# An eighth weight home and a last expert added on the chip in a two-layer mixture-of-experts kernel

## What is computed

```python
def expert_choice_ffn(h, router_w, router_b, w_gate, w_up, w_down):
    cap = EC_CAPACITY * n // N_EXPERTS            # 64 latent rows, 32 context rows
    affinity = jax.nn.softmax(h @ router_w + router_b)
    gates, idx = lax.top_k(jnp.swapaxes(affinity, 1, 2), cap)
    xg = h[idx]
    hid = silu(xg @ w_gate[e]) * (xg @ w_up[e])
    y = (hid @ w_down[e]) * gates[..., None]
    return zeros.at[idx].add(y)                   # summed over the experts

for l in range(DEPTH):                            # DEPTH = 2
    ...
    f_l = expert_choice_ffn(modulate(rmsnorm(x, norm_ffn_pre[l]), mod_l[3], mod_l[4]), ...)
    x = x + mod_l[5] * rmsnorm(f_l, norm_ffn_post[l])
    if l < DEPTH - 1:                             # the context takes part in layer 0 only
        ctx = ctx + mod_c[5] * rmsnorm(expert_choice_ffn(..ctx..), norm_ffn_post[l])
return x
```

## Time and profile before

| | |
|---|---|
| median of 3 executions | 2183.53 us (2183.09 to 2184.22) |
| the profiled execution, its own time | 2187.91 us |
| its span, first to last instruction | 2186.1 us |
| mean granted clock of TensorE | 0.943 of full speed |
| PE busy | 1913.0 us, 88% |
| DVE busy | 633.0 us, 29% |
| ACT busy | 504.2 us, 23% |
| POOL busy | 208.6 us, 10% |

### The profile page before, as it was taken

One profiled execution on the slowest core, in us unless ns is written; L12 is line 12 of the kernel. 1 busy time (PEld: TensorE's weight loads), 2 busy tenths in 40 slices (PEclk: granted clock), 3 DMA queues, 4 the chain that ended last, 5 costly groups with the idle time before them and its releaser, 6 DMA issues. The chain is left out here.

```text
span 2186.1 us, 25132 instructions
## 1 busy us (share of the span) xinstructions
PE 1913.0 (88%) x10556; PEld 916.3 (42%) x10556; DVE 633.0 (29%) x1195; ACT 504.2 (23%) x999; POOL 208.6 (10%) x225
## 2 busy tenths in 40 slices
PE   5998999989979999999995999999694978778775
PEld 2656555434423333333333766655342323222221
DVE  2257542352331111111105356523523100000002
ACT  3145541442200000000005145514221100000002
POOL 2300000210011110111111000001100100000000
PEclk9999999989989999999997999999796999888988
DMA  9520305111279999999998123014317999999997
GB/s 350 165 77 1 135 1 180 52 41 76 90 296 400 394 395 399 394 399 395 395 395 307 39 77 135 1 60 172 136 47 292 403 398 406 401 400 406 401 401 268
DMA packets 166976, 534.51 MB, mean 245 GB/s; under 512 B 11208, under 2 KB 19730, under 8 KB 166866
## 3 DMA queue, kind: packets, MB, share of 16 engines
q1 hardware_dynamic: 148720, 487.40, 57.3%
q0 software_dynamic: 16480, 40.21, 6.5%
q10 hardware_dynamic: 1666, 5.31, 0.7%
HBM read 507.72 MB, written 25.17 MB: 244 GB/s over the span
## 5 line engine op out<-in xcount | busy, mean ns | idle before, releaser
L2766 PE MATMUL ps<-ring,arena 128*64 128x512 f32 x1040 | 244.6, 624 | 36.2 <-DMA ring<-in_w_up 33.1
L2766 PE MATMUL ps<-arena 128*64 128x512 f32 x840 | 199.4, 626 | 36.4 <-DMA arena<-in_w_up 36.4
L2105 PE MATMUL ps<-arena,ring 128*128 128x256 f32 (+1 forms) x640 | 202.8, 479 | 5.9 <-DMA ring<-in_w_in 3.0
L2105 PEld LDWEIGHTS ps<-arena,ring 128*128 128x128 f32 x640 | 123.2, 194 | 86.3 <-issue 70.1
L2766 PEld LDWEIGHTS ps<-ring,arena 128*64 128x64 f32 x1040 | 79.5, 143 | 188.5 <-issue 184.8
L2023 DVE TENSOR_TENSOR arena<-arena,ps 128x512 f32<-128x512 f32 x32 | 22.0, 687 | 439.7 <-ACT arena L1302 439.7
L2614 PE MATMUL ps<-ring,arena 128*128 128x512 f32 x320 | 142.8, 601 | 2.2 <-DVE arena L1940 1.8
L789 POOL DMA_INDIRECT expert_sums<-arena,small x32 | 51.6, 1611 | 839.2 <-ACT arena L1309 839.2
L2766 PEld LDWEIGHTS ps<-arena 128*64 128x64 f32 x840 | 64.3, 144 | 160.2 <-issue 160.2
L1302 ACT ACTIVATE arena<-ps 128x512 f32<-128x512 f32 x32 | 19.1, 597 | 453.9 <-PE ps L2766 453.9
L2809 PE MATMUL ps<-ring,arena 128*64 128x512 f32 x496 | 111.3, 594 | 2.8 <-DMA ring<-in_w_down 2.1
(11 more groups left out here) (352 smaller groups left out, 2404.5 us busy)
## 6 DMA issues: line engine op xcount, KB each, us to landing
ring<-in_w_up SPq DMA_DIRECT2D x33, 2048.0 KB, 18.4
ring<-in_w_gate SPq DMA_DIRECT2D x32, 2048.0 KB, 23.3
ring<-in_w_down SPq DMA_DIRECT2D x31, 2048.0 KB, 24.5
ring<-in_ada_w SPq DMA_DIRECT2D x24, 2048.0 KB, 12.9
arena<-in_w_down SPq DMA_DIRECT2D x21, 2048.0 KB, 25.2
arena<-in_w_gate SPq DMA_DIRECT2D x19, 2048.0 KB, 22.7
arena<-in_w_up SPq DMA_DIRECT2D x18, 2048.0 KB, 17.1
ring<-in_w_in SPq DMA_DIRECT2D x6, 2048.0 KB, 15.9
```

Of the source, the lines that this page charges most:

```text
L2105: ins = mm(o[0:n, c0:c1], w[:, k, col:col + n], hT[:, k, c0:c1], start=k == 0, stop=k == KD - 1)
L2766: ins = mm(px[0][hf * 64:hf * 64 + 64, col:col + 512], xl[e % 2][:, at:at + CAP_L], w[c][:, hf * 512:hf * 512 + 512], start=b + c == 0, st ...
```

## The change

It has six parts. (1) In layer 0, `tail_job` has another order. (2) Layer 0 gets an eighth home. It consists of three pieces, one of them `mrows`, which the mixing stage still uses, so that its first load waits for ACT's and DVE's marks after the choice of rows; `sg_l` and one of two `hT_l` go. (3) PE's first experts in layer 0 come in another order. (4) POOL adds an expert's context rows ahead of its latent rows, and DVE modulates the context rows of expert 1 ahead of the latent rows of expert 0. (5) In layer 1 gate blocks are let go on a semaphore of their own, `gate_used`, after the gate products and not after the up products. (6) At the end of layer 1 the sums of 15 experts are loaded from HBM. The sixteenth's rows are added by products: for each tile of 128 tokens PSUM receives identity x sums plus a 0/1 matrix x rows, where the matrix (`last_hits`) compares numbers of slots (`last_no`, loaded from the constants) with the row's number. ACT and DVE read the sum from PSUM. The last gate's rows are formed before the last down stage.

```diff
-XRING = [RING + EXTRA] * (DEPTH - 1) + [len(LAST_HOMES)]
+XRING = [RING + EXTRA + 1] * (DEPTH - 1) + [len(LAST_HOMES)]
...
-        order += [("mix", c + 1)] * (c + 1 < n) + [("ctx", 0)] * (early and c == 3) + [("out", c)]
-        order += [("turn", c - 1)] * (c >= 1) + [("ctx", c - 3)] * (early and c > 3)
+        order += [("mix", c + 1)] * (c + 1 < n) + [("ctx", 0), ("ctx", 1)] * (early and c == 4) + [("out", c)]
+        order += [("turn", c - 1)] * (c >= 1) + [("ctx", 2)] * (early and c == 4)
...
-            let_go += [("blocks_used", n)] * 2 + [("gu_lat", e + 1)] * 2
+            if l < DEPTH - 1:
+                let_go += [("blocks_used", n)] * 2 + [("gu_lat", e + 1)] * 2
+            else:
+                let_go += [("gate_used", 2 * e + 1), ("blocks_used", n), ("gate_used", 2 * e + 2), ("gu_lat", e + 1)]
...
+        extra_homes = [((0, 4, extra[i]),) for i in range(EXTRA)]
+        extra_homes += [((0, 2, ar(20480, 2048)), (2, 3, mrows[:, :]), (3, 4, ar(m0 + 3584, 1024)))]
...
-                    elif home == "d":
+                    elif home == "d" or (l < DEPTH - 1 and home == RING + EXTRA):
                         for s in (dve_ph, act_ph):
                             sp.wait_ge(s, PHASES * l + CHOICE_DONE)
...
-                pool.wait_ge(S["y_lat"], l * NE + e + 1)
-                pool.indirect_dma_start(halves_sum[l], at_rows(e, 0), y_l[e % 2], None, compute_op=ALU.add)\
-                    .then_inc(put_lat, 16)
                 if ctx_on:
                     pool.wait_ge(S["y_ctx"], l * NE + e + 1)
                     pool.indirect_dma_start(quarters_sum[l], at_rows(e, NE), y_c[e % 2], None, compute_op=ALU.add)\
                         .then_inc(put_ctx, 16)
+                pool.wait_ge(S["y_lat"], l * NE + e + 1)
+                pool.indirect_dma_start(halves_sum[l], at_rows(e, 0), y_l[e % 2], None, compute_op=ALU.add)\
+                    .then_inc(put_lat, 16)
...
-                add_rows(l, NE - 1)
+                    if l == DEPTH - 1 and e == NE + 1:
+                        pool.wait_ge(S["down_lat"], l * NE + NE - 2)
+                        load(last_no, T["const"][:, K_END:K_END + SEQ], s_no)
+                if l < DEPTH - 1:
+                    add_rows(l, NE - 1)
...
                 latent_rows_turned(0)
+                if ctx_on:
+                    pe.wait_ge(S["rows_mod"], n0 + 2)
+                    pe.wait_ge(S["hid_ctx"], n0 + 1)
+                    n = BLOCKS[l].index((0, 1, 0))
+                    context_gate_up(1, 0, block(n), block(n + 1))
...
+                def last_sums_up(i, t):
+
+                    o, no = last_sums(t), last_hits[:, i * P:(i + 1) * P]
+                    pe.wait_ge(sum_loaded[t], 16 * (l + 1))
+                    for hf in range(2):
+                        mm(o[:, hf * 512:(hf + 1) * 512], ident, Fa[:, t, hf * 512:(hf + 1) * 512], start=True, stop=False)
+                    pe.wait_ge(S["y_lat"], n0 + NE)
+                    for hf in range(2):
+                        half = slice(hf * CAP_L, (hf + 1) * CAP_L)
+                        ins = mm(o[:, hf * 512:(hf + 1) * 512], no[half, :], y_l[(NE - 1) % 2][half, :], start=False, stop=True)
+                    ins.then_inc(S["sums_full"], 1)
```

183 lines of the change are left out of this document (108 added, 75 removed).

## The result

The changed kernel takes 2189.55 us (median of 20 executions, 2182.92 to 2196.21); the kernel before, in 20 executions beside it, 2184.65 us. The ratio is 1.0021, with a 95% interval of 1.0013 to 1.0029: slower by some 4.6 us, where I had forecast no difference (2183.0, range 2176 to 2189). The change moves the time little, but not because it does little: in the profiled executions (spans 2186.07 and 2189.55) it gives 12.6 us away in one place and gets 9.1 back, net, in the others.

The account below looks back on a forecast made before the run. In layer 0's experts PE and the weight stream were taken to run neck and neck, in layer 1's the stream alone; 11.9 - 2.85 - 1.1 - 3.5 - 5.0 = -0.55 from 2183.53 gave 2183.0 us, range 2176 to 2189.

Parts of the forecast that it names:

- Term A: Start of layer 0's experts: PE waits for block 7 and block 12 is issued late; 11.9 us slower.
- T: Layer 0's start: the moment when the first half of `gate_up(0)` ends, forecast at 646.8 us.
- doesn't repay it: Layer 0's experts: an eighth home gives nothing to a stream whose DMA share is 1.03.
- Term B: Tail of layer 0: the third `out_half` loses its slot wait and the half clock behind it; 2.85 us faster.
- Term C: Handover to layer 1: the context's scatter-add, issued ahead of the latent one, leaves the chain; 1.1 us faster.
- Term D: Layer 1's start: gate blocks let go after gate products restart the stream sooner; 3.5 us faster.
- Term E: End of layer 1: sums of 15 experts loaded early, the last rows added by products; 5.0 us faster.
- Last rows 2163.0: End of layer 1: the last rows come at 2163.0 us, the constants' load costing the stream 0.6, hidden.
- The end gives little: Rival, end of layer 1: slow fifteenth scatter-add or half-clock products, gain only 1.8 to 3 us; 15 in 100.
- Layer 0 stays bound by PE: Rival, layer 0's experts: only PE's own shift counts, +4.6 us, time 2175.7 us; 25 in 100.
- Block 7 lands late: Rival, layer 0's start: block 7 lands after 634.4 us, at 643.4 giving 2192.0 us; 15 in 100.
- the gate semaphore does nothing: Rival, layer 1's start: the earlier release gains 0, time 2186.6 us, no difference; 5 in 100.

Follow-up runs that it names:

- seven homes: The basis, but layer 0 has seven homes as before; 2176.92 us, ratio 0.9961.
- the basis: The changed kernel with PE's old order at layer 0's start and the last gate's rows ahead of the last up stage; 2174.15 us, ratio 0.9949.
- gate with up: The basis, but in layer 1 the gate blocks are let go with the up blocks again; 2174.76 us, ratio 0.9953.
- old end: The basis, but with the end of layer 1 as before: sixteen scatter-adds, sums loaded after the last, no products; 2174.64 us, ratio 0.9955.
- layer 0 only: The basis, but with layer 1's gate blocks let go with the up blocks and its end as before; 2179.14 us, ratio 0.9964.
- early gate rows: The changed kernel with the last gate's rows ahead of the last up stage and DVE's diagonal before the 0/1 matrix; 2186.78 us, ratio 0.9992.

## Why the prediction was wrong

**Term A (11.9) was right, in mechanism and size.** 12.6 measured, the landing of block 7, T and the issue of block 12 within 0.2 us of the forecast (PE's wait was 5.1 and not 6.1, because PE came to it a microsecond later), and the two orders tried apart give their shares. What it lacked: 1.0 us because the context's down ran slower than in the earlier trace rows; and the sentence that the eighth home "doesn't repay it" is wrong at the handover, where seven homes bring the sums' load 1.9 us later ("seven homes" against the basis).

**Term B's tail (2.85)** came as forecast (2.95). The cut by itself moves by more than that, but the rows bear it out: the wait of 1.85 is gone, the third `out_half` took 8.80 us before and takes 7.03 now, and the wait that I had put at 0.7 is found at 0.64:

```profile
557.95 7.11 PE L2647 MATMUL ps<-ring,arena 128*128 128x512 f32 x16 [0.64 <-ACT arena L1268]
```

But 0.5 to 1.7 of it is lost again at the context's down, which I had booked nowhere.

**Term C (1.1)** gave 2.1 at the sums' first load (10.84 and 8.75 us behind the last down), 0.8 at the opening products of layer 1 and 0.4 up to its experts; tried alone, the order of the scatter-adds is worth 1.6 at the sums' load.

**Term D (3.5)** gave 4.7; half clock had lengthened before's group more than after's (9.89 against 8.62). At like clock it gives 3.45, in two pairs of kernels (10.10 and 6.65; 8.49 and 5.04).

**Term E (5.0) is the step that failed**: 1.8 at the end, less 0.75 for the constants' load, which I had called hidden. From the first waiting load to the last up stage the three kernels without that load took 450.4 to 450.6 us, all others 451.1 to 451.8. From the last weighting to the first square the term was right: 4.38 us (forecast 4.65) where it was 9.65, 5.27 gained. What failed stands on either side of it. "Last rows 2163.0" let the stream set the last down; in the changed kernel PE sets it, and the last weighting starts 26.1 us after the cut at the last up stage and not 24.0, 2.1 later. And "DVE's chain behind it, 2.46 us a tile, stays": it goes at PE's pace of up to 2.98, and from the first square to the end it takes 1.35 more. 2.13 + 1.35 - 5.27 is the -1.79 of the table.

Under both lies one misreading. The sentence was "the first tile then takes four products. At full clock (0.43 each)". I had taken "x4" in the row of the gate rows for four products. `gate_rows` has two, as the order's rows do (x2): the trace keeps two records for each float32 product of 128 rows by 512 columns. At full clock one takes 0.98, not 0.43 (L2901: 1.95 for two). So the gate rows hold PE for 1.98 us and not 0.9, and a tile takes 2.95 and not 1.7, which is more than DVE's 2.46. The Trainium skill, "FP8 and Floating Point Precision", section "TensorE Precision Notes", says that a true float32 product passes the array four times; as an estimate, 4 x 512 columns at 2.4 GHz are 0.85 us, which is near L2901's 0.98 and would have caught the misreading. The two products of the 0/1 matrix, with 64 rows each, take 1.06 together, about half as much (from 2172.20 to 2173.26): they read different halves of the rows. The Trainium skill, "TensorEngine Tiling (Array Packing)", section "When to Use Tiling", names a contract dimension of 64 as a case for two tiles of rows; the 1.06 agrees with it.

The half clock in the last up stage, 1.7 us, is the other half of the late last down. Of the 14 profiled kernels nine had it, and before's, the basis, "gate with up", "old end" and "layer 0 only" had not. By itself it costs 0.1 us at the last down (with early gate rows), because PE then merely waits less for blocks 94 and 95. The gate rows alone at full clock would cost an estimated 0.4 (26.1 less 1.7, against 23.9 to 24.0); no run shows that. Both together are more than those waits can take up.

**The rivals.** "The end gives little" had the right place and nearly the right size (-1.8 to -3), but the wrong cause: the products ran at full clock, and the fifteenth scatter-add took 4.8 us, not 8.0. "Layer 0 stays bound by PE" has fallen for the changed kernel; in the windows from 700 to 1150 us the stream stood at 392 to 401 GB/s, as before, and not at the ceiling of the ports, 435 GB/s in the Trainium skill, "DMA: Bandwidth & Descriptors", section "Where 436 GB/s comes from". "Block 7 lands late" and "the gate semaphore does nothing" have fallen. The sum with E at its measured size, 2183.0 + 4.0 = 2187.0, would have been inside the range; 2.5 us remain, of which 0.7 is term A and the rest lies within what the medians of before moved from one series of measurements to another (2184.65 to 2187.76).

**Open:** the timing gives the release and the old end 1 us each, the traces 3.45 and 4.3, and for both together 3 to 5 stand against 7. With the uncertainty of 4 these don't contradict each other, and only more executions of each kernel would tell. Why one execution has half clock in the last up stage and another not is open, too.

## What to carry to other kernels

When a stream of loads is within a per cent of the engine that it feeds, ask of each reordering which home it lets go later, and find the first load that waits for it: one home let go 17 us later cost 6 us, and with the second reorder, which made PE wait for block 7, it was 12.6, though PE had the same work. A stream's last block matters beyond the stage: what is issued behind it (here scatter-adds and the loads of their sums) lands later while it runs. Work put on an engine that waits for a stream is free only as far as those waits reach: here the half clock fitted into them, and with the gate rows on top the last down came 2.1 us late. And before pricing a product from a trace's row, divide the row by the number of products that the code has there, not by its count of records.

## What was unexpected of the hardware

A scatter-add of 64 chosen latent rows, in halves of 512, took 5.3 to 5.9 us to land when the weight stream ended within 5.6 us of the last down, and 7.5 to 8.2 us when it ran on to 10.5 to 11.5 us. An extra home thus brought the next step, the load of the sums, 1.9 us forward, beside the 1.85 us of PE's one wait for a block. The second half of the last up stage, behind a wait of 1.4 to 5.0 us, ran at 2.4 GHz throughout in the profiled executions of five kernels (7.09 us) and in part at 1.2 GHz in those of nine (8.78 us). Kernels with the same instructions there are in both groups, so this difference of 1.7 us goes with no edit of that stage.
